# A second mixer whose values are the weights of its products, and ropes ahead of the weight halves, in a one-core encoder block

## The chip, the cores and the metric

One core of a Trainium2 chip runs the whole kernel in one launch. The metric is the device time of that launch in microseconds (us); lower is better.

## The reference, cut to what matters

One encoder block on 256 tokens of 1024 features. With n = RMSNorm(x), one wide projection gives queries, keys, values and gates of two attention mixers:

```python
[qA|kA|vA|qB|kB|vB|gA|gB] = n @ W_in
yA = DifferentialAttention(qA, kA, vA)      # 4 heads, rotary on 16 of 64 features, sub-norm
yB = softmax(SCALE * qB @ kB.T + bias) @ vB # 8 heads of 64 features, windowed by a bias
x = x + (sigmoid(gA) * (yA @ W_pA) + sigmoid(gB) * (yB @ W_pB)) @ W_out
x = x + PEER(RMSNorm(x))                    # 16384 experts, 16 of 256 candidates per head
out = RMSNorm(x)
```

The second mixer's softmax divides each row of exponentials by its sum before the product with the values; the kernel may divide before or after that product.

## The kernel before

**Work.** The weights come as a stream of 128-row tiles (128 partitions x 8 x 128 numbers, 512 KB each). Tile k is a slot: 0 to 3 are qA, 4 to 7 kA, 8 to 11 vA, 12 to 15 qB, 16 to 19 kB, 20 to 23 vB, 24 to 39 the gates (T_PROJ = 40), then 8 projections, 8 of W_out, 16 of the expert queries, 128 of expert inputs (U) and 128 of expert outputs (V). Every product is made of halves: ScalarE copies a raw tile to a rounded high half (`whi`, L475), VectorE subtracts it from the raw tile to get the low half (`wlo`, L699), and TensorE adds three products for each of 8 chunks, 24 matmuls of 256 columns a tile (L1156, one call of `tile`). The halves of tile t are made LEAD = 3 slots ahead, in slot t - 3, in a ring of 4. Tiles of values are taken in pairs (`token_pair`), 48 matmuls, and such a pair waits for the low halves of both of its tiles (L1330).

**Order.** Every engine's queue is an order written out by hand: a loop over the slots k, in which each engine's steps stand one behind another. An engine runs its queue strictly in that order, so a wait holds up all behind it.

- SyncE issues the loads (L377). Load t waits for the low half of tile t - 4 (L376).
- ScalarE, slot k: high half of tile k + 3 (L515), then for k < 8 the copy of the product of slot k out of PSUM (L519), which waits for that product. In slot 3 follow a square root (L521) and an exponential with a load of its table (L523). From slot 12 come the units' steps.
- VectorE, slot k < 12: low half of tile k + 3 (L818), then in slot 3 the norm (L716, L718), in slots 5, 6, 9 and 10 the four parts of the two ropes (L826; `ROPE_AT`, L79): part (0,0) makes two tables with cosine and sine times 1/rms (L806, L807), shuffles and multiplies (L809, L810), part (0,1) multiplies and adds (L812, L813), and (1,0) and (1,1) do the same for the keys. The queries' factor SCALE is in their tables.
- TensorE, slot k: the tile, then `scores`, `turn`, `times_v`. The first scores (slot 12) wait for both ropes (L1215).

**The opening.** `two_tiles` (L1276) runs tiles 0 and 1 in a mixed order as halves of x and weights arrive; tile 1's first product waits for the whole high half of tile 1 (L1307). In it, `rest(0, c)` are the products with the low half of x.

**Units.** Each mixer has 8 units (a head or pair of heads for 128 queries). Unit n starts in its slot: 12 to 19 for the first mixer, 25 to 32 for the second. In the second mixer, lag 0: scores on TensorE (L1221, two matmuls that use 64 rows of the array each), scale and bias and maximum on VectorE (L857, L860), exponentials with their sums on ScalarE (L550). Lag 1: 1/sum on VectorE (L846). Lag 2: four transposes of the probabilities (L1240) and their copy (L769). Lag 3: `times_v`, four matmuls with the turned probabilities as weights and 64 columns of values moving (L1258), result with queries on partitions, and VectorE multiplies it with 1/sum into `oB` (L774). In slots 37 and 38 (`Y_AT`, L88) `turn_y(2)` and `turn_y(3)` transpose `oB` (L1273, four transposes each), and `y_parts` makes halves `yhi`, `ylo` of it for the projections. The first mixer ends in `oA`, turned in slots 25 and 26.

An fp32 matmul shows as two records in the trace, a transpose as one.

## Time and profile before

| | |
|---|---|
| median of 3 runs | 1013.02 us (1012.43 to 1013.66) |
| the profiled execution | 1012.58 us |
| its span, first to last instruction | 1010.7 us |
| TensorE, matmuls | 1000.9 us busy, 99% |
| VectorE | 839.9 us, 83% |
| ScalarE | 604.9 us, 60% |
| mean granted TensorE clock | 0.998 of full speed |

The profiled execution's own time is 1.9 us above its span, which is what lies around the first and last instruction. Times in the rows below are us from the span's start. In a timeline, neighbouring instructions of one form are merged, and the bracket names the idle time of the engine ahead of them and what ended it. The chain is followed back from the last instruction through what released each step. Ends of matmuls are modelled, their starts are recorded.

### The profile page before, as it was taken

The numbers are of one execution on the slowest core, as the hardware profiler recorded it, in microseconds if no ns is written. First come the engines' busy times: TensorE is split into PE (matmuls) and PEld (weight loads), VectorE is DVE, ScalarE is ACT, GpSimd is POOL, SyncE is SP. The second block draws the span as 40 slices with busy tenths as digits, with TensorE's granted clock in tenths as the row PEclk, the third lists the DMA queues.
The fourth block names the chain that finished last, engine by engine and source line by source line (L and its number), as shares of the span: only waits on it lengthen the run. The fifth ranks groups of instructions, "written<-read, shape, count | busy, mean of one in ns | idle before, by whom it ended". The sixth has DMA issues, their size and how long they took to land.

```text
span 1010.7 us, 20524 instructions
## 1 busy us (share of the span) xinstructions
PE 1000.9 (99%) x6945; PEld 921.6 (91%) x6945; DVE 839.9 (83%) x1674; ACT 604.9 (60%) x1144; POOL 81.0 (8%) x38
## 2 busy tenths in 40 slices
PE   8999999999999999999999999999999999999997
PEld 8889999999999999999999999978888888888886
DVE  7888869769998989999999999777777777777776
ACT  6456544655545468888888888544444444444444
POOL 0000000277860000000000000000000000000000
PEclk9999999999999999999999999999999999999999
DMA  8744445645677766666666666887777777777772
GB/s 296 232 141 147 126 138 175 230 161 200 197 235 231 236 208 213 208 209 208 198 216 208 202 206 212 274 311 236 235 236 233 235 234 234 233 235 235 234 232 73
DMA packets 87749, 214.93 MB, mean 213 GB/s; under 512 B 9728, under 2 KB 43008, under 8 KB 87296
## 3 DMA queue, kind: packets, MB, share of 16 engines
q1 hardware_dynamic: 87104, 213.07, 65.3%
q8 instruction: 45, 0.74, 0.3%
q10 hardware_dynamic: 576, 0.93, 0.3%
q14 instruction: 24, 0.20, 0.1%
HBM read 195.08 MB, written 18.87 MB: 212 GB/s over the span
## 4 chain that ended last, share of the span: by engine, by line
PE 97%; DVE 1%; DMA 1%; issue 0%; ACT 0%; ACTq 0%
PE pO L1156 36%; PE pO L1441 18%; PE pTT L1473 17%; PE pM L1473 17%; PE pSS L1415 1%; PE pTT L1415 1%; DMA raw<-in_stream 1%; PE pSS L1221 1%; PE pSS L1379 1%; PE pM L1258 1%; PE pTT L1240 0%; PE pTT L1484 0%; PE pM L1252 0%; PE pTT L1233 0%; DVE wlos L699 0%
## 5 line engine op out<-in xcount | busy, mean ns | idle before, releaser
L475 ACT ACTIVATE whis<-raw 128x1024 fp32r<-128x1024 f32 x327 | 345.5, 1057 | 203.3 <-PE pM L1473 172.8
L1064 DVE TENSOR_TENSOR wlos<-raw,whis 128x1024 fp32r<-128x1024 f32 x125 | 153.3, 1226 | 87.5 <-ACT whis L475 87.4
L699 DVE TENSOR_TENSOR wlos<-raw,whis 128x1024 fp32r<-128x1024 f32 x169 | 205.1, 1219 | 14.7 <-ACT whis L475 14.2
L1156 PE MATMUL pO<-xhi,whis 128*128 128x256 f32 x752 | 212.2, 282 | 0.8 <-ACT qkT L519 0.8
L1156 PE MATMUL pO<-xlo,whis 128*128 128x256 f32 x752 | 210.0, 279 | 0.0
L1156 PE MATMUL pO<-xhi,wlos 128*128 128x256 f32 x752 | 209.8, 279 | 0.0
L1441 PE MATMUL pO<-xlo,whis 128*128 128x256 f32 x512 | 143.4, 280 | 0.0
L1156 PEld LDWEIGHTS pO<-xhi,whis 128*128 128x128 f32 x752 | 141.2, 188 | 2.2 <-issue 1.8
L1441 PE MATMUL pO<-xhi,wlos 128*128 128x256 f32 x512 | 143.0, 279 | 0.0
L1441 PE MATMUL pO<-xhi,whis 128*128 128x256 f32 x512 | 143.0, 279 | 0.0
L1156 PEld LDWEIGHTS pO<-xlo,whis 128*128 128x128 f32 x752 | 141.3, 188 | 0.0
L1156 PEld LDWEIGHTS pO<-xhi,wlos 128*128 128x128 f32 x752 | 140.9, 187 | 0.0
L602 ACT ACTIVATE ast<-pO 128x256 f32<-128x256 f32 x128 | 49.1, 384 | 100.5 <-PE pO L1156 69.6
L461 POOL TENSOR_TENSOR wlos<-raw,whis 128x1024 fp32r<-128x1024 f32 x33 | 80.6, 2447 | 216.2 <-ACT whis L475 216.1
L1441 PEld LDWEIGHTS pO<-xlo,whis 128*128 128x128 f32 x512 | 96.4, 188 | 0.0
L1441 PEld LDWEIGHTS pO<-xhi,wlos 128*128 128x128 f32 x512 | 96.1, 188 | 0.0
L1441 PEld LDWEIGHTS pO<-xhi,whis 128*128 128x128 f32 x512 | 95.9, 187 | 0.0
L610 ACT ACTIVATE ghot<-ghot,routeT 128x128 fp32r<-128x128 f32 x256 | 88.3, 397 | 5.4 <-DVE ghot L1043 5.4
L1055 DVE TENSOR_TENSOR wfull<-aring,G 128x256 f32<-128x256 f32 x128 | 78.9, 617 | 0.0
L1473 PE MATMUL pTT<-whis,ghi 128*128 128x512 f32 x250 | 78.7, 396 | 0.0
L1473 PE MATMUL pTT<-whis,glo 128*128 128x512 f32 x250 | 78.6, 396 | 0.0
L1473 PE MATMUL pM<-whis,glo 128*128 128x512 f32 x250 | 78.6, 395 | 0.0
(251 smaller groups left out, 1867.1 us busy)
## 6 DMA issues: line engine op xcount, KB each, us to landing
raw<-in_stream SPq DMA_DIRECT2D x199, 512.0 KB, 3.7
raw<-in_vrows SPq DMA_DIRECT2D x128, 512.0 KB, 3.5
a_scratch<-ast SPq DMA_DIRECT2D x128, 128.0 KB, 1.9
aring<-a_scratch SPq DMA_DIRECT2D x128, 128.0 KB, 3.3
biasm<-in_bias SPq DMA_DIRECT2D x8, 256.0 KB, 5.4
keysT<-in_keys SPq DMA_DIRECT2D x1, 1024.0 KB, 6.2
h_scratch<-h1tok SPq DMA_DIRECT2D x1, 1024.0 KB, 6.5
htok<-h_scratch SPq DMA_DIRECT2D x1, 1024.0 KB, 9.8
```

The source lines that it names most:

```text
L461: pool.tensor_tensor(wlo[s], raw[s][:], whi[s].bitcast(F32), ALU.subtract).then_inc(lo_ready, 1)
L475: act.activation(whi[s], raw[s][:], ACT.Copy).then_inc(hi_ready, 1)
L602: act.activation(ast[i % 2][:], pO[i % 2][:, 0:T], ACT.Gelu).then_inc(evac_act, 1)
L610: last = act.activation(ghot[:, u % HOTS, tok, 1, :], ghot[:, u % HOTS, tok, 0, :].bitcast(F32), ACT.Copy, scale=routeT[:, 2, at:at + 1])
L699: dve.tensor_tensor(wlo[t % RING], raw[t % RING][:], whi[t % RING].bitcast(F32), ALU.subtract).then_inc(lo_ready, 1)
L1055: dve.tensor_tensor(wfull[s % 2][:], aring[s][:], mine.rearrange("p t o -> p (t o)"), ALU.mult).then_inc(w_ready, 1)
L1064: dve.tensor_tensor(wlo[s], raw[s][:], whi[s].bitcast(F32), ALU.subtract).then_inc(lo_ready, 1)
L1156: last = pe.matmul(dst, st, mv, start=(c == 0 and q == 0), stop=(c == len(terms) - 1 and q == 2))
L1221: last = pe.matmul(pS[m][:, 0:T], qkT[rows, q0 + h, b * P:(b + 1) * P], qkT[rows, k0 + h, :], start=True, stop=True)
L1415: last = pe.matmul(pG[k % 2][:, p, tok * 2 * P:(tok + 1) * 2 * P], hot1[:, u % HOTS, tok, :], ghot[:, u % HOTS, tok].rearrange("p h i -> p ...
L1441: last = pe.matmul(pO[i % 2][:, 0:T], st[s][:, c, :], mv[:, c, :], start=c == 0 and q == 0, stop=c == C - 1 and q == 2)
L1473: last = pe.matmul(acc[b][q], st, mv[:, q * 512:(q + 1) * 512], start=first and n == 0, stop=n == 2 and (b, q) == closed)
```

## The change

It does seven things.

1. ScalarE makes the high half of tile 1 in two halves of four chunks, with a semaphore of its own for the first (`second_hi`), and TensorE starts tile 1 on the first. In `two_tiles` the `rest(0, c)` are spread otherwise (from chunk 5 on).
2. ScalarE's copy of product k goes ahead of the high half of tile k + 3, for product 0 ahead of the squares and of the high half of tile 3. It scales the queries of the first mixer by SCALE.
3. VectorE's rope parts go ahead of the low half of tile k + 3 in slots 5, 6, 9 and 10. The tables have no SCALE in them, and are made once, for the queries, and used again for the keys.
4. In the second mixer, ScalarE multiplies the probabilities with 1/sum in lag 1, two activations a unit, before they are turned. The transposes wait for them.
5. `times_v` of the second mixer has the values as weights (64 columns) and the turned probabilities moving (128 columns). The two heads of a pair write partitions 0 to 63 and 64 to 127, and alternate.
6. ScalarE copies that result from PSUM to `yhi` (in the slot after the product), and VectorE subtracts to `ylo` (`pair_low`), in place of the multiplication into `oB`.
7. `turn_y(2)`, `turn_y(3)` and their `y_parts` are gone.

```diff
@@ -85,7 +85,7 @@
 WHOLE_LAG = 2
 HALF = C // 2
 RCOL_AT = 6
-Y_AT = {T_GATE + 1: 0, T_GATE + 2: 1, T_PROJ - 3: 2, T_PROJ - 2: 3}
+Y_AT = {T_GATE + 1: 0, T_GATE + 2: 1}
 
 GTOK = 4
 GSUB = 2
@@ -506,17 +511,25 @@
             for c in range(C):
                 act.wait_ge(x_landed[c // 2], 16)
                 gained_hi(0, c)
-            hi_at(1)
+            def raw_copy(k):
+
+                act.wait_ge(tile_done, k + 1)
+                act.activation(qkT[:, k, :], pO[k % 2][:, 0:T], ACT.Copy, scale=SCALE if k < HA else 1.0).then_inc(evac_act, 1)
+
+            for half in range(2):
+                part = slice(half * HALF, (half + 1) * HALF)
+                act.wait_ge(raw_landed[1], 16)
+                act.activation(whi[1][:, part], raw[1][:, part], ACT.Copy).then_inc(hi_ready if half else second_hi, 1)
             hi_at(2)
+            raw_copy(0)
             act.activation(gates[:, 0:C // 2, :], xT[:, 0:C // 2, :], ACT.Square).then_inc(squares, 1)
             hi_at(3)
             for k in range(T_PROJ):
+                if 0 < k < T_VA:
+                    raw_copy(k)
                 if k:
                     hi_at(k + LEAD)
                 if k < T_VA:
-
-                    act.wait_ge(tile_done, k + 1)
-                    act.activation(qkT[:, k, :], pO[k % 2][:, 0:T], ACT.Copy).then_inc(evac_act, 1)
                     if k == 3:
                         rms_root(1)
                         act.wait_ge(lam_sums, 1)
@@ -537,6 +550,14 @@
                         act.wait_ge(pv_done, n + 1)
                         act.activation(gates[:, n // 2, n % 2 * P:(n % 2 + 1) * P], pM[n % 2][:, 0:P], ACT.Square, accum_out=ssA[:, 1, n:n + 1])
                         act.activation(oA[:, n // HA, n % HA, :], pM[n % 2][:, 0:P], ACT.Copy).then_inc(pv_taken, 1)
+                    else:
+                        act.wait_ge(pv_done, n + 1)
+                        act.activation(yhi[:, HA + (n - UNITS_A) % HA, (n - UNITS_A) // HA * P:((n - UNITS_A) // HA + 1) * P], pM[n % 2][:, 0:P], ACT.Copy).then_inc(yb_hi, 1)
+                for n in units_at(k, 1):
+                    if n >= UNITS_A:
+                        act.wait_ge(inverse_ready, n - UNITS_A + 1)
+                        for m in range(2):
+                            act.activation(prob[:, n % 2, m, :], prob[:, n % 2, m, :], ACT.Copy, scale=rz[:, n, m:m + 1]).then_inc(prob_normed, 1)
                 for n in units_at(k, 0):
                     act.wait_ge(max_ready, n + 1)
                     if n >= 2:
@@ -555,8 +576,7 @@
                 if k in Y_AT:
                     j = Y_AT[k]
                     act.wait_ge(y_full, j + 1)
-                    half, b = j // 2, j % 2
-                    act.activation(yhi[:, half * HA:(half + 1) * HA, b * P:(b + 1) * P], yf[:], ACT.Copy).then_inc(y_hi, 1)
+                    act.activation(yhi[:, 0:HA, j * P:(j + 1) * P], yf[:], ACT.Copy).then_inc(y_hi, 1)
             for k in range(T_PROJ, T_QUERY):
                 hi_at(k + LEAD)
                 if k == T_PROJ:
@@ -768,28 +788,23 @@
                 w = T if n < UNITS_A else 2 * T
                 dve.tensor_copy(probT[:, n % 2, 0:w], pT[n % 2][:, 0:w]).then_inc(turned_taken, 1)
 
-            def take_pv(n):
-                dve.wait_ge(pv_done, n + 1)
-                h, b = (n - UNITS_A) % HA, (n - UNITS_A) // HA
-                dve.tensor_tensor(oB[:, b, h, :].rearrange("p (m v) -> p m v", m=2),
-                                  pM[n % 2][:, 0:P].rearrange("p (m v) -> p m v", m=2),
-                                  rz[:, n, :].unsqueeze(2).to_broadcast([P, 2, DH]), ALU.mult).then_inc(pv_taken, 1)
+            def pair_low(n):
+
+                u = n - UNITS_A
+                dve.wait_ge(yb_hi, u + 1)
+                at = (slice(None), HA + u % HA, slice(u // HA * P, (u // HA + 1) * P))
+                dve.tensor_tensor(ylo[at], pM[n % 2][:, 0:P], yhi[at].bitcast(F32), ALU.subtract).then_inc(yb_lo, 1)
 
             def y_parts(j, t):
 
-                half, b = j // 2, j % 2
                 dve.wait_ge(y_turned, j + 1)
                 if j:
                     dve.wait_ge(y_lo, j)
-                src = pT[j % 2].rearrange("p (h t) -> p h t", h=HA)
-                if half == 0:
-                    dve.tensor_scalar(yf[:], src, lam[:, 6:7], None, ALU.mult).then_inc(y_full, 1)
-                else:
-                    dve.tensor_copy(yf[:], src).then_inc(y_full, 1)
+                dve.tensor_scalar(yf[:], pT[j % 2].rearrange("p (h t) -> p h t", h=HA), lam[:, 6:7], None, ALU.mult).then_inc(y_full, 1)
                 low_front(t)
                 dve.wait_ge(y_full, j + 1)
                 dve.wait_ge(y_hi, j + 1)
-                at = (slice(None), slice(half * HA, (half + 1) * HA), slice(b * P, (b + 1) * P))
+                at = (slice(None), slice(0, HA), slice(j * P, (j + 1) * P))
                 dve.tensor_tensor(ylo[at], yf[:], yhi[at].bitcast(F32), ALU.subtract).then_inc(y_lo, 1)
 
             bview = biasm[:].rearrange("p b h (r c) -> p b (h r) c", c=GRID_W)
@@ -802,9 +817,9 @@
                 turned = oB[:].rearrange("p b h v -> p (b h v)")
                 turned3 = turned.rearrange("p (h t) -> p h t", t=T)
                 if part == 0:
-                    scale = 1.0 if half else SCALE
-                    link(dve.scalar_tensor_tensor(tables[:, 0, :], K("cos"), scale, rstd[:], ALU.mult, ALU.mult))
-                    link(dve.scalar_tensor_tensor(tables[:, 1, :], K("sin"), scale, rstd[:], ALU.mult, ALU.mult))
+                    if half == 0:
+                        dve.tensor_tensor(tables[:, 0, :], K("cos"), rstd[:], ALU.mult)
+                        link(dve.tensor_tensor(tables[:, 1, :], K("sin"), rstd[:], ALU.mult))
                     dve.wait_ge(evac_act, (half + 1) * HA)
                     link(dve.stream_shuffle(turned, raws.rearrange("p h t -> p (h t)"), ROTATED))
                     link(dve.tensor_tensor(turned3, turned3, tables[:, 1, :].unsqueeze(1).to_broadcast([P, HA, T]), ALU.mult))
@@ -814,6 +829,8 @@
                     dve.wait_ge(roped, half + 1)
 
             for k in range(T_PROJ + 1):
+                if k in ROPE_AT:
+                    rope(*ROPE_AT[k])
                 if 0 < k < T_QB:
                     low_front(k + LEAD)
                 if k == 1:
@@ -822,8 +839,6 @@
                     rms(1)
                 if k == 5:
                     lambda_rest()
-                if k in ROPE_AT:
-                    rope(*ROPE_AT[k])
                 if k == RCOL_AT:
                     dve.wait_ge(rstd_turned, 1)
                     dve.tensor_copy(rcol[:], pTT[:, :, 0:1].rearrange("p b o -> p (b o)")).then_inc(rcol_ready, 1)
@@ -831,6 +846,9 @@
                     dve.wait_ge(tile_done, k + 1)
                     taken = qkT[:, k - T_QB + 8, :] if k < T_VB else gates[:, k - T_GATE, :]
                     dve.tensor_tensor(taken, pO[k % 2][:, 0:T], rstd[:], ALU.mult).then_inc(evac_dve, 1)
+                for n in units_at(k - 1, 3):
+                    if n >= UNITS_A:
+                        pair_low(n)
                 for n in units_at(k, 1):
                     dve.wait_ge(exp_done, 2 * (n + 1))
                     if n < UNITS_A:
@@ -843,7 +861,7 @@
                                                  ALU.mult, ALU.add).then_inc(dif_ready, 1)
                         dve.wait_ge(dif_ready, n + 1)
                     else:
-                        link(dve.reciprocal(rz[:, n, :], zs[:, n, :]))
+                        dve.reciprocal(rz[:, n, :], zs[:, n, :]).then_inc(inverse_ready, 1)
                 for n in units_at(k, 0):
                     dve.wait_ge(scores_done, n + 1)
                     if n < UNITS_A:
@@ -860,9 +878,6 @@
                         dve.tensor_reduce(nmx[:, n, :], prob[:, n % 2, :, :], AX_X, ALU.max, negate=True).then_inc(max_ready, 1)
                 for n in units_at(k, 2):
                     take_turned(n)
-                for n in units_at(k, 3):
-                    if n >= UNITS_A:
-                        take_pv(n)
                 if T_QB <= k < T_PROJ and k not in Y_AT:
                     low_front(k + LEAD)
                 if T_VB <= k < T_GATE:
@@ -1232,7 +1247,7 @@
                     for kb in range(TB):
                         last = pe.transpose(pT[n % 2][:, kb * P:(kb + 1) * P], dif[:, n % 2, kb * P:(kb + 1) * P], ident)
                 else:
-                    pe.wait_ge(exp_done, 2 * (n + 1))
+                    pe.wait_ge(prob_normed, 2 * (n - UNITS_A + 1))
                     if n < UNITS_A + 2:
                         pe.wait_ge(y_full, 2)
                     for m in range(2):
@@ -1242,8 +1257,10 @@
 
             def times_v(n):
                 pe.wait_ge(turned_taken, n + 1)
-                if n >= 2:
+                if 2 <= n < UNITS_A + 2:
                     pe.wait_ge(pv_taken, n - 1)
+                elif n >= 2:
+                    pe.wait_ge(yb_lo, n - 1 - UNITS_A)
                 last = None
                 if n == 0:
                     pe.wait_ge(evac_act, evac_engine(T_QB - 1)[1])
@@ -1253,24 +1270,19 @@
                                          start=kb == 0, stop=kb == TB - 1)
                 else:
                     pair = (n - UNITS_A) % HA
-                    for m in range(2):
-                        for kb in range(TB):
-                            last = pe.matmul(pM[n % 2][:, m * DH:(m + 1) * DH], probT[:, n % 2, m * T + kb * P:m * T + (kb + 1) * P],
-                                             vtok[:, kb, HA + pair, m * DH:(m + 1) * DH], start=kb == 0, stop=kb == TB - 1)
+                    for kb in range(TB):
+                        for m in range(2):
+                            last = pe.matmul(pM[n % 2][m * DH:(m + 1) * DH, 0:P], vtok[:, kb, HA + pair, m * DH:(m + 1) * DH],
+                                             probT[:, n % 2, m * T + kb * P:m * T + (kb + 1) * P], start=kb == 0, stop=kb == TB - 1)
                 last.then_inc(pv_done, 1)
 
             def turn_y(j):
-                half, b = j // 2, j % 2
-                if half == 0:
+                if j == 0:
                     pe.wait_ge(y_ready, 1)
                     pe.wait_ge(turned_taken, UNITS_A)
-                else:
-                    pe.wait_ge(pv_taken, UNITS_A + UNITS_B)
-                    pe.wait_ge(turned_taken, UNITS_A + UNITS_B)
-                src = oA if half == 0 else oB
                 last = None
                 for h in range(HA):
-                    last = pe.transpose(pT[j % 2][:, h * P:(h + 1) * P], src[:, b, h, :], ident)
+                    last = pe.transpose(pT[j][:, h * P:(h + 1) * P], oA[:, j, h, :], ident)
                 last.then_inc(y_turned, 1)
 
             def two_tiles():
@@ -1300,12 +1312,15 @@
                     pe.wait_ge(gain_hi, c + 1)
                     high(0, c)
                     low(0, c)
-                    if c >= C - 2:
-                        rest(0, c - (C - 2))
-                for c in range(2, C - 2):
+                    if c > HALF:
+                        rest(0, c - HALF - 1)
+                for c in range(C - HALF - 1, C - 2):
                     rest(0, c)
-                pe.wait_ge(hi_ready, 1)
                 for c in range(C):
+                    if c == 0:
+                        pe.wait_ge(second_hi, 1)
+                    elif c == HALF:
+                        pe.wait_ge(hi_ready, 1)
                     high(1, c)
                 for c in range(C - 2, C):
                     last = rest(0, c, c == C - 1)
@@ -1351,10 +1366,8 @@
                 if k == T_GATE + 1:
                     turn_y(0)
                     turn_y(1)
-                if k in (T_PROJ - 3, T_PROJ - 2):
-                    turn_y(k - T_PROJ + 5)
-            pe.wait_ge(y_lo, 4)
-            pe.wait_ge(y_hi, 4)
+            pe.wait_ge(y_lo, TB)
+            pe.wait_ge(yb_lo, UNITS_B)
             for k in range(T_PROJ, T_OUT):
                 tile_wait(k)
                 s = k % RING
```

The parts left out declare semaphores: `second_hi`, `inverse_ready`, `prob_normed`, `yb_hi` and `yb_lo`.

## Rows read from the trace of the kernel before

**Rows 1.** The page: span, and the chain that ended last, by engine.
```profile
span 1010.7 us, 20524 instructions
...
PE 97%; DVE 1%; DMA 1%; issue 0%; ACT 0%; ACTq 0%
```

**Rows 2.** Waits of TensorE: waiting line <- awaited line: us in total, times, longest.
```profile
PE pSS L1221 <- DVE qkT L813: 1.4, 1, 1.4
```

**Rows 3.** Timeline of TensorE, 0 to 50 us: start, duration, what, idle before.
```profile
13.69 0.36 PE L1156 MATMUL pO<-xhi,whis 128*128 128x256 f32 x1 [0.66 <-ACT qkT L519]
...
16.83 0.36 PE L1156 MATMUL pO<-xhi,whis 128*128 128x256 f32 x1 [0.18 <-ACT qkT L519]
...
47.52 0.70 PE L1221 MATMUL pSS<-qkT 64*128 64x256 f32 x4 [1.45 <-DVE qkT L813]
```

**Rows 4.** Timeline of ScalarE, 8 to 40 us, same columns.
```profile
17.84 1.06 ACT L475 ACTIVATE whis<-raw 128x1024 fp32r<-128x1024 f32 x1
19.84 0.38 ACT L519 ACTIVATE qkT<-pO 128x256 f32<-128x256 f32 x1 [0.93 <-PE pO L1156]
...
21.89 1.28 ACT L523 ACT_TABLE_LOAD   x1
...
23.30 1.04 ACT L475 ACTIVATE whis<-raw 128x1024 fp32r<-128x1024 f32 x1
```

**Rows 5.** Timeline of VectorE, 14 to 48 us, same columns.
```profile
14.69 1.22 DVE L699 TENSOR_TENSOR wlos<-raw,whis 128x1024 fp32r<-128x1024 f32 x1
...
18.73 2.35 DVE L699 TENSOR_TENSOR wlos<-raw,whis 128x1024 fp32r<-128x1024 f32 x2
...
24.44 2.38 DVE L699 TENSOR_TENSOR wlos<-raw,whis 128x1024 fp32r<-128x1024 f32 x2 [0.78 <-ACT whis L475]
...
30.84 1.22 DVE L699 TENSOR_TENSOR wlos<-raw,whis 128x1024 fp32r<-128x1024 f32 x1
31.98 1.22 DVE L812 TENSOR_TENSOR qkT<-qkT,mfull 128x1024 f32<-128x1024 f32 x1
33.23 1.23 DVE L813 TENSOR_TENSOR qkT<-qkT,oB 128x1024 f32<-128x1024 f32 x1
```

**Rows 6.** Chain that ended last, 20 to 50 us: start, duration, what.
```profile
32.21 5.72 PE pO L1156 x48
...
38.01 1.07 ACT whis L475
...
46.24 1.24 DVE qkT L813
```

**Rows 7.** Timeline of TensorE: the first matmuls and the last.
```profile
1.00 3.13 PE L1322 MATMUL pM<-ones 128*128 128x128 f32 x13 [1.00 <-POOL ones L456]
...
1005.08 0.28 PE L1484 MATMUL pO<-whis,glo 128*128 128x256 f32 x1
```

**Rows 8.** Window: PE, PEld, DVE, ACT, POOL busy, PEclk, DMA share, GB/s.
```profile
1007.00:1008.00 1.00, 0.00 (x0) 0.00 (x0) 0.54 (x1) 0.42 (x1) 0.00 (x0) 0.75 0.00 0
```

**Rows 9.** Chain that ended last, 94 to 152 us: tile, product, tile, turn.
```profile
100.26 2.92 PE pO L1156 x24
...
118.34 0.84 PE pM L1258 x8
119.18 2.88 PE pO L1156 x24
...
146.82 0.44 PE pTT L1273 x4
```

**Rows 10.** Chain that ended last, 52 to 66 us: scores, product, tile.
```profile
58.53 0.63 PE pSS L1221 x4
...
59.53 0.45 PE pM L1252 x4
59.98 2.73 PE pO L1156 x24
```

**Rows 11.** Timeline of ScalarE, 118 to 127 us: the wait ahead of the exponentials.
```profile
124.87 0.51 ACT L550 ACTIVATE prob<-prob,nmx 128x256 f32<-128x256 f32 x1 [2.59 <-DVE nmx L860]
```

More of the change, by code:

```diff
@@ L272, in build @@
         head_landed = sem("head_landed")
+        second_hi = sem("second_hi")
         head_hi = sem("head_hi")
@@ L320, in build @@
         y_lo = sem("y_lo")
+        inverse_ready = sem("inverse_ready")
+        prob_normed = sem("prob_normed")
+        yb_hi = sem("yb_hi")
+        yb_lo = sem("yb_lo")
         m_full = sem("m_full")
```

## The prediction

> **What bounds the kernel now.** I read the page first, for the span and the engines' shares of the chain that ended last; then the waits of TensorE, which show where that engine is not the bound; then the timelines of the first 50 us, where the change reorders queues; then the chain in the second mixer, where it changes matmuls. TensorE holds 97% of the chain [rows 1]. So whatever changes its own work or its waits passes to the end, one for one. Its longest wait is 1.4 us, at the first scores, for VectorE's ropes [rows 2]. The others are small and lie in the first 33 us [rows 3]. Less work on ScalarE or VectorE gains nothing by itself; a later half of a tile can cost.
>
> **Part 1, the opening.** Tile 2 starts at 13.69 after 0.66 of idle time, for ScalarE's copy of product 0, which stands behind the high half of tile 3 [rows 3]. With the copy ahead, and tile 1 started on its first four chunks, tile 2 could start at about 12.4. I take this as a gain of 1.3 us that doesn't last: tile 3 needs its low half, which VectorE begins at 14.69 for 1.22 us [rows 5], untouched by the edits. So tile 3 starts at about 15.95 and not 16.83 [rows 3], and 0.9 us is left. This is work ahead of the next wait, and is lost in it.
>
> **Part 2, copies ahead of high halves.** The high half of tile 6 starts at 17.84, the copy of product 3 at 19.84 [rows 4], 3.01 us after tile 3's start at 16.83 [rows 3]. In the new order the half stands behind that copy. Tile 3 starts at 15.95, so the copy runs at 18.96; 0.3 us on, the half runs from 19.25 to 20.3. VectorE makes two low halves (tiles 5 and 6) in 2.35 us from 18.73 [rows 5]; now the second waits, and ends at 21.5 in place of 21.0. Behind it come the norm, the root and the table load (before: 21.89 for 1.28 us), then the exponential and the copy of product 4 (0.3 us, now first), then the high half of tile 7, before at 23.30 [rows 4]. It moves by 0.5 + 0.3 = 0.8 us, to 24.1, and so does the low half of tile 7 behind it, from 24.44 [rows 5] to 25.24.
>
> **Part 3, ropes ahead of low halves.** From 24.44 to 34.5 VectorE has no idle time, so everything queued there adds up. The pair of tiles 8 and 9 needs the low half of tile 9, which runs from 30.84 to 32.06 [rows 5], and TensorE starts the pair at 32.21 [rows 6]. Now rope part (0,1) goes ahead of that half: two operations, 31.98 to 34.46, with the step between them 2.5 us [rows 5]. Rope (0,0) trades places with the low half of tile 8 and changes no sum. Low half of tile 9: 32.06 + 0.8 + 2.5 = 35.36; the pair starts at 35.5. TensorE is earlier until then: from 15.95 it has five tiles (3 to 7) of 2.73 to 2.92 us [rows 9, 10] and two small groups, so tile 7 ends at about 30.7. It would stand idle for 4.8 us, where its longest wait was 1.4 [rows 2]. Queued behind are all later tiles.
>
> The pair takes 5.72 us [rows 6], then come the second pair and tile 12. The first scores start at 47.52 after 1.45 us of idle time [rows 3], so from the pair's start to the end of tile 12 it is 47.52 - 1.45 - 32.21 = 13.86 us. New end of tile 12: 49.36. Are the ropes there by then? The high half of tile 12 follows the pair's end (before: 38.01, 5.80 after its start [rows 6]), so it runs at 41.3 to 42.35 and the low half to 43.6. Rope (1,0) has no tables now and is done before, since it stands ahead of that low half. Rope (1,1) takes 2.5 us like (0,1) (its last operation before: 46.24 [rows 6]), and ends at 46.1. So the scores don't wait: they start at 49.36 against 47.52 [rows 3], **+1.8 us**. The old wait of 1.45 us has gone, and a wait of 4.8 us stands in an earlier place.
>
> Loads: SyncE issues load t when low half t - 4 is done, so loads 13 to 15 go out about 3 us later. Their high halves, behind the pairs, move by as much. No DMA is added, and none is moved past another.
>
> **Part 4, the clock.** The last matmul starts at 1005.08 [rows 7], and in the window 1007 to 1008 the mean granted clock is 0.75 [rows 8]: it fell to the lower level (1.2 GHz) 2.1 us after TensorE stopped (half of that window at full speed, half at 0.5). At the start, the first 13 records of 128 columns took 3.13 us [rows 7], 0.21 each; four such records take 0.45 us later, 0.11 each [rows 10]. So after a cold start TensorE ran at half speed for 3 us. A stall of 1.45 us showed no such thing in its tiles. One of 4.8 us lies well above both, so I take it that the clock falls and that the pair begins with 3 us at 1.2 GHz: **+1.5 us** (bounds: 0, if it holds, and 2.9, half of the pair, if it stays low through it). With this, tile 12 ends at 50.9, the pair at 42.8, the ropes at 47.6: still ahead of the scores.
>
> **Part 5, the turns that go.** `turn_y(2)` and `turn_y(3)` are 4 transposes each, 0.44 us [rows 9], on the chain: **-0.9 us**. Their copies on VectorE and ScalarE were beside the tiles.
>
> **Part 6, values as weights.** Before: 8 records a unit, 0.84 us [rows 9]. After: 8 records of 128 columns. No row shows matmuls on two column halves. The nearest are the scores, on two row halves: 4 records of 256 columns in 0.63 us [rows 10]. By the 0.112 us of a 128-column record [rows 10], four in a row would be 0.90, two at a time 0.45; so they run two at a time, with 0.18 us for going in and out. For the new product: 4 x 0.112 + 0.18 = 0.63, and 0.04 more on the tile behind (2.92 behind scores, 2.88 behind the old product [rows 9]), 0.67. That saves 0.17 x 8 = **-1.4 us**. Lower bound, nothing for in and out: 0.45, -3.1 us. Upper bound, one column half after the other: 0.90 + 0.22 = 1.12, +2.2 us.
>
> **Part 7, the new steps beside TensorE.** ScalarE gets two 256-column activations a unit, 0.38 us each (the copy at 19.84 [rows 4]), and one of 128 columns, at most as much: 1.1 us. It waits 2.59 us in such a slot for VectorE's maximum [rows 11], and all three fit ahead of that. VectorE's `pair_low` replaces an operation of the same size. It waits for ScalarE's copy, and the scale and bias of the next unit are queued behind it; the copy has had a slot's time. The turn of a unit comes one slot after the scaling. I cost all of this at nothing. Were it all on the path, it would be 8 x 1.1 = 9 us, which the cover of 2.59 excludes.
>
> **Sum.** 1.8 + 1.5 - 0.9 - 1.4 = +1.0 us on the profiled execution's 1012.58: 1013.6. The median of the runs is 0.44 above that execution, so I say 1014.0 against 1013.02, which is +0.1%. A measurement of this kernel tells about 0.2% (2 us) from no change.
>
> **Rivals.**
>
> Slower: *the column halves take turns.* Place: the 8 products. Price: +2.2 in place of -1.4, total +4.6, 1017.6. It decides once a product costs 0.13 us more than I say, 0.80 against 0.67. For it: the scores' halves use different rows of the array, these share the rows. Against it: adjacent matmuls alternate between the halves, as in the scores. The Trainium skill bears on this in "TensorE: Matmul & The Clock Gate", Part 3: it says that a weight load overlaps with a running matmul only where the row group differs. By that rule each load of 64 columns stands open here, which by the page's P / 1.2 is 53 ns, 8 a unit, an estimate of 0.42 us a unit, and the total would be 8 x 0.42 above mine, +4.4. The same part reports gains from packing by columns, and no row of this trace can settle it.
>
> Faster: *the clock holds and tiles run short.* Some tiles of 24 matmuls last 2.73 us [rows 10] and others 2.83 to 2.9 [rows 9], 0.1 us apart, with no wait in either; every tile behind an old product was a long one. If those behind the new product were short, up to the end of the projections, that is 19 tiles, -1.9 us. Alone it gives -0.9, or 1012.1, no change. With a clock that holds (-1.5) it gives -2.4, 1010.6. Against the second part: the fall in rows 8 after 2.1 us.
>
> No change in another way: *the clock alone holds*, -0.5, 1012.5. That would follow if the stall were under 2 us, say if TensorE reached the pair later than I think.
>
> That the edits don't act as they say is a small risk: the opening's gain is real, and I hold that all of it is lost in the stall.
>
> **How the numbers follow.** Forecast and its neighbours within 2 us (clock falls or holds, columns in pairs): 0.51. Columns in turns or a longer spell of low clock: 0.32, slower. Short tiles with a clock that holds, or products near their lower bound: 0.17, faster. The range goes from the faster rival, 1010.6, to the slower one, 1017.6; the unchanged case alone is 1012.1 to 1015.
>
> **What would show it.** (a) An idle time of 4 to 5 us on TensorE ahead of the pair of tiles 8 and 9, ended by VectorE's low half at about 35.4; below 2 us would mean that I have VectorE's queue wrong. (b) Records twice as far apart for some 3 us behind it. (c) No wait at the first scores. (d) Tile 2 at about 12.4, tile 3 at about 16. (e) The new product in about 0.65 us, its records in pairs with nearly one start; single starts 0.11 apart would be the slower rival. (f) No turns at slots 37 and 38. (g) ScalarE's wait ahead of the exponentials shorter by about 1 us, and still there. I am wrong if the time is below 1011 or above 1017.6.

## The result, and the profile after

The changed kernel takes **1014.74 us** (median of 20, 1013.83 to 1015.32), the kernel before beside it 1013.0 (20 runs). The ratio is 1.0016, 95% interval 1.001 to 1.0023. The kernel became slower by 1.7 us, which is clear of the noise and within the 0.2% that the prediction called no change. The profiled execution took 1014.73 us, 2.15 more than the one of before.

The page: span, TensorE's busy time, engines of the chain.

```profile
span 1012.9 us, 20516 instructions
...
PE 1001.0 (99%) x6937; PEld 919.8 (91%) x6937; DVE 836.7 (83%) x1668; ACT 612.3 (60%) x1167; POOL 80.8 (8%) x38
...
PE 96%; DVE 2%; DMA 1%; ACT 1%; issue 0%; SPq 0%; DVEq 0%
```

Against [rows 1] the span is 2.2 us longer. TensorE's share of the chain fell from 97% to 96%.

The waits of TensorE (left out: 1.0 us ahead of its first matmul):

```profile
PE pO L1171 <- DVE wlos L719: 4.8, 2, 4.5
...
PE pO L1293 <- ACT xhi L492: 0.6, 1, 0.6
```

The wait of [rows 2], for the ropes at the first scores, is gone. In its place stand 4.8 us of waits for a low half of a tile, 4.5 of them at one place. The timelines show where. TensorE first: start, duration, what, and in brackets the idle time before it.

```profile
16.14 0.39 PE L1171 MATMUL pO<-xhi,whis 128*128 128x256 f32 x1 [0.36 <-DVE wlos L719]
...
35.68 0.55 PE L1171 MATMUL pO<-whis,xhi 128*128 128x256 f32 x1 [4.48 <-DVE wlos L719]
```

Tile 3 starts at 16.14 (before: 16.83 [rows 3]) and the pair of tiles 8 and 9 at 35.68 (32.21 [rows 6]). ScalarE in the same stretch:

```profile
19.27 0.38 ACT L517 ACTIVATE qkT<-pO 128x256 f32<-128x256 f32 x1 [2.10 <-PE pO L1171]
19.55 1.05 ACT L480 ACTIVATE whis<-raw 128x1024 fp32r<-128x1024 f32 x1
...
24.34 1.05 ACT L480 ACTIVATE whis<-raw 128x1024 fp32r<-128x1024 f32 x1
```

The copy of product 3 waits 2.10 us for its product, and the high half of tile 6 stands behind it: 19.55 where it was 17.84, and the half of tile 7 comes at 24.34, where it was 23.30 [rows 4]. VectorE:

```profile
20.64 1.23 DVE L719 TENSOR_TENSOR wlos<-raw,whis 128x1024 fp32r<-128x1024 f32 x1 [0.51 <-ACT whis L480]
...
25.49 1.23 DVE L719 TENSOR_TENSOR wlos<-raw,whis 128x1024 fp32r<-128x1024 f32 x1 [1.05 <-ACT whis L480]
...
31.79 1.23 DVE L827 TENSOR_TENSOR qkT<-qkT,mfull 128x1024 f32<-128x1024 f32 x1
33.05 1.23 DVE L828 TENSOR_TENSOR qkT<-qkT,oB 128x1024 f32<-128x1024 f32 x1
34.31 1.23 DVE L719 TENSOR_TENSOR wlos<-raw,whis 128x1024 fp32r<-128x1024 f32 x1
```

The low half of tile 7 starts at 25.49 (before 24.44 [rows 5]). The second rope part of the queries, 31.79 and 33.05, stands ahead of the low half of tile 9, which therefore runs from 34.31 and not from 30.84. That half is what the pair waits for.

Behind the stall comes the second cost. Windows of 1 us: the window, its length, then the busy time and count of TensorE, of its weight loads, of VectorE, ScalarE and GpSimd, then the mean granted clock, DMA share and GB/s.

```profile
35.00:36.00 1.00, 0.32 (x1) 0.35 (x2) 1.00 (x3) 0.00 (x0) 0.00 (x0) 0.80 0.02 8
36.00:37.00 1.00, 1.00 (x6) 1.00 (x6) 1.00 (x2) 0.00 (x0) 0.00 (x0) 0.50 0.56 82
...
38.00:39.00 1.00, 1.00 (x6) 1.00 (x6) 1.00 (x1) 0.00 (x0) 0.00 (x0) 0.50 1.08 334
39.00:40.00 1.00, 1.00 (x11) 1.00 (x10) 0.96 (x2) 0.00 (x0) 0.00 (x0) 1.00 1.01 191
```

The granted clock is 0.5 (1.2 GHz) when the pair starts, and until about 39.0. By their starts, the matmuls are 0.213 us apart until then and 0.118 us behind it. The chain through the rest of the opening:

```profile
35.68 15.87 PE pO L1171 x120
51.55 0.63 PE pSS L1236 x4
```

The first scores start at 51.48 by the timeline, 3.96 us later than the 47.52 of [rows 3]. Then the second mixer; the chain gives transposes, product, tile and scores of one unit, and the last run of tiles:

```profile
116.55 0.59 PE pTT L1255 x4
117.13 0.59 PE pM L1275 x8
117.72 3.02 PE pO L1171 x24
120.74 0.63 PE pSS L1236 x4
...
143.94 8.09 PE pO L1171 x67
```

The product takes 0.59 us and took 0.84 [rows 9], but the tile behind it takes 3.02 and took 2.88. The period of a slot is 4.83 against 4.94. After the last product there is no turn: `pO L1171` runs on without one.

A piece of the chain begins where the one before it ends, and these ends are modelled. The recorded starts of transposes, product and tile, before and after, divide the change otherwise:

```profile
117.68 0.66 PE L1240 MATMUL pTT<-cst,prob 128*128 128x128 f32 x4
118.17 1.00 PE L1258 MATMUL pM<-vtok,probT 128*128 128x64 f32 x8
118.99 0.37 PE L1156 MATMUL pO<-xhi,whis 128*128 128x256 f32 x1
```

```profile
111.65 0.66 PE L1255 MATMUL pTT<-cst,prob 128*128 128x128 f32 x4
...
112.82 0.39 PE L1171 MATMUL pO<-xhi,whis 128*128 128x256 f32 x1
```

From the product's start, 112.23 in the changed kernel, to the tile's it is 0.59 us and was 0.82, a gain of 0.23. From the first transpose's start to the product's it is 0.58 and was 0.49, a loss of 0.09 ahead of the product. Behind it the tile loses only about 0.02. The product's first records on TensorE, two that start together, and its weight loads with the next one behind them:

```profile
112.23 0.33 PE L1275 MATMUL pM<-probT,vtok 128*64 128x128 f32 x2
```

```profile
112.23 0.42 PEld L1275 LDWEIGHTS pM<-probT,vtok 128*64 128x64 f32 x8 [0.17 <-issue]
112.82 0.19 PEld L1171 LDWEIGHTS pO<-xhi,whis 128*128 128x128 f32 x1 [0.17 <-issue]
```

Eight loads of 64 columns lie in 0.42 us; each end of the group has 0.17 us in which no load runs, put down to issue. ScalarE's new steps in such a slot, and its wait ahead of the exponentials:

```profile
120.94 0.26 ACT L555 ACTIVATE yhi<-pM 128x128 fp32r<-128x128 f32 x1
121.62 0.91 ACT L560 ACTIVATE prob<-prob,rz 128x256 f32<-128x256 f32 x2 [0.43 <-DVE rz L864]
123.52 0.51 ACT L571 ACTIVATE prob<-prob,nmx 128x256 f32<-128x256 f32 x1 [0.98 <-DVE nmx L878]
```

The wait is 0.98 us, where it was 2.59 [rows 11]. The new steps take 0.26 and 0.91 us, and there is a new wait of 0.43 us for 1/sum. A wait is still left ahead of the exponentials, so these steps cost nothing at the end.

The balance of the profiled execution: +3.96 at the first scores, -0.11 in the first mixer's stage (second mixer's first scores: 98.92 us against 95.07), then about -0.9 for the products and -0.9 for the turns. The first product of the output stage starts at 177.81 against 175.73, 2.08 later, and the last matmul 2.14 later.

### The profile page after: what moved, and what is told of

The parts are those of the page before. It is cut to its first block, busy times and chain, and to the rows that moved or that the text cites. A ratio compares the mean times of both kernels' runs of the same rounds, so it can differ in the third digit from the quotient of the medians.

```text
span 1012.9 us, 20516 instructions
## 1 busy us (share of the span) xinstructions
PE 1001.0 (99%) x6937; PEld 919.8 (91%) x6937; DVE 836.7 (83%) x1668; ACT 612.3 (60%) x1167; POOL 80.8 (8%) x38
## 4 chain that ended last, share of the span: by engine, by line
PE 96%; DVE 2%; DMA 1%; ACT 1%; issue 0%; SPq 0%; DVEq 0%
PE pO L1171 36%; PE pO L1454 18%; PE pTT L1486 17%; PE pM L1486 17%; PE pSS L1428 1%; PE pTT L1428 1%; PE pSS L1236 1%; DVE wlos L719 1%; PE pSS L1392 1%; DMA raw<-in_stream 1%; PE pM L1275 0%; PE pTT L1255 0%; PE pTT L1497 0%; PE pM L1269 0%; PE pTT L1248 0%
## 5 line engine op out<-in xcount | busy, mean ns | idle before, releaser
L1171 PE MATMUL pO<-xhi,whis 128*128 128x256 f32 x752 | 212.2, 282 | 0.4 <-DVE wlos L719 0.4
L1171 PE MATMUL pO<-xlo,whis 128*128 128x256 f32 x752 | 210.0, 279 | 0.0
L1171 PE MATMUL pO<-xhi,wlos 128*128 128x256 f32 x752 | 209.8, 279 | 0.0
L1171 PEld LDWEIGHTS pO<-xhi,whis 128*128 128x128 f32 x752 | 141.1, 188 | 3.0 <-issue 2.0
L1171 PEld LDWEIGHTS pO<-xlo,whis 128*128 128x128 f32 x752 | 141.3, 188 | 0.0
L1171 PEld LDWEIGHTS pO<-xhi,wlos 128*128 128x128 f32 x752 | 140.9, 187 | 0.0
```

The costliest lines, as they stand in the source:

```text
L1171: last = pe.matmul(dst, st, mv, start=(c == 0 and q == 0), stop=(c == len(terms) - 1 and q == 2))
```

## The experiments

Each time stands beside the kernel before, run on the same chip: 1012.78 us for e1 to e4 and again for e7 to e9, 1012.85 for e5 and e6. The changed kernel's 1014.74 stands beside 1013.0, 0.2 us more, so a difference from it can be off by that much.

**e1: ropes back behind the low halves.**

```diff
-                if k in ROPE_AT:
-                    rope(*ROPE_AT[k])
                 if 0 < k < T_QB:
                     low_front(k + LEAD)
...
                 if k == 5:
                     lambda_rest()
+                if k in ROPE_AT:
+                    rope(*ROPE_AT[k])
```

> The changed kernel with the rope parts back behind the low halves; copies of the products stay ahead. Stall theory (VectorE's order makes the stall, and the stall makes the low clock): the pair of tiles 8 and 9 starts at about 33.4 us instead of 35.7, after some 2.4 us of idle time; the first scores come at about 47.8 instead of 51.5; time about 1011.5 if the clock holds, 1013 if it falls. Rival (the high halves that stand behind the copies are the cause): the pair stays at about 35.5 us and the time near 1014.7.

Measured: 1012.18 us, ratio 0.9988 (0.9978 to 0.9997). Two lines of TensorE's timeline, the pair and the first scores, then a window:

```profile
33.05 0.36 PE L1171 MATMUL pO<-whis,xhi 128*128 128x256 f32 x1 [2.06 <-DVE wlos L719]
```

```profile
47.37 0.70 PE L1236 MATMUL pSS<-qkT 64*128 64x256 f32 x4 [0.46 <-DVE qkT L828]
```

```profile
33.00:34.00 1.00, 0.95 (x8) 0.98 (x9) 1.00 (x1) 0.30 (x1) 0.00 (x0) 1.00 0.42 104
```

The idle time is 2.06 us, the pair starts at 33.05 and the first scores at 47.37. In the profiled execution the clock held; it took 1010.53 us. The ten executions lie in two groups, four from 1010.5 to 1011.0 and six from 1012.1 to 1012.6. The gap fits a clock that falls in some of them; their mean granted clocks point that way (0.998 to 1.0 in the four, 0.997 or 0.998 in the six) but overlap. So VectorE's order is the larger part of the stall, and the rival, the copies alone, is refuted.

**e2: the kernel before with ropes ahead, and nothing else.**

```diff
+                if k in ROPE_AT:
+                    rope(*ROPE_AT[k])
                 if 0 < k < T_QB:
                     low_front(k + LEAD)
...
-                if k in ROPE_AT:
-                    rope(*ROPE_AT[k])
```

> The kernel before with one edit, the rope parts ahead of the low halves. Stall theory: idle time of about 3 us ahead of the pair of tiles 8 and 9, which starts at about 34.7 us; 1.1 us later at the first scores if the clock holds, 3.2 us later if it falls to 1.2 GHz; time 1014.1 or 1016.2, I expect the latter. Rival (only ropes and copies together cost): no change, 1013.

Measured: 1015.17 us, ratio 1.0017 (1.0008 to 1.0027), 2.4 us more than the kernel before; ten executions, three from 1013.3 to 1013.6 and seven from 1015.0 to 1016.3. Timeline, then windows, of the profiled one (1015.05):

```profile
34.76 0.36 PE L1156 MATMUL pO<-whis,xhi 128*128 128x256 f32 x1 [3.26 <-DVE wlos L699]
```

```profile
35.00:36.00 1.00, 1.00 (x10) 1.00 (x10) 1.00 (x2) 0.00 (x0) 0.00 (x0) 0.86 0.37 53
36.00:37.00 1.00, 1.00 (x6) 1.00 (x6) 1.00 (x2) 0.00 (x0) 0.00 (x0) 0.50 0.89 295
```

Here the clock was still full when the pair started and fell 1 us later, at about 35.7, though TensorE was busy again. So one edit to one queue makes the stall and the low clock by itself. I had expected 1016.2; the median lies 1 us lower, and three executions, with a mean granted clock of 0.999, lie below the 1014.1 expected for a held clock. Behind the low clock come these starts, 95 steps apart:

```profile
39.17 0.28 PE L1156 MATMUL pO<-whis,xhi 128*128 128x256 f32 x1
...
49.95 0.28 PE L1156 MATMUL pO<-xhi,wlos 128*128 128x256 f32 x1
```

That is 0.1135 us a matmul, where the changed kernel had 0.118 behind its own low clock.

**e3: the stall filled.**

```diff
+                if k == T_VA - 1:
+                    for _ in range(18):
+                        pe.matmul(pM[1][:, 0:P], ones[:], ones[:], start=True, stop=True)
```

> The changed kernel with 18 matmuls on ones (128 columns, 4.0 us in all) in the stall behind tile 7; their result is used by nothing. The stall stays as long; only its emptiness goes. Clock theory: the granted clock stays at full speed and the pair's first 3.3 us aren't run at half speed: 1.7 us less, 1013.0 (1012.6 if the pair also runs at the shorter spacing). Rival (the time is lost to the wait alone and the low clock costs nothing at the end): 1014.7.

Measured: 1012.54 us, 2.2 less than the changed kernel's 1014.74; ratio 0.9997 (0.9988 to 1.0007), which makes it 1.9. Timeline and a window:

```profile
35.35 0.36 PE L1171 MATMUL pO<-whis,xhi 128*128 128x256 f32 x1 [0.46 <-DVE wlos L719]
```

```profile
36.00:37.00 1.00, 1.00 (x11) 1.00 (x10) 1.00 (x2) 0.00 (x0) 0.00 (x0) 1.00 0.57 111
```

The pair starts at 35.35, hardly earlier, the clock stays, and the first scores start at 49.13, 2.35 us ahead of the changed kernel. Of these, 0.33 are the earlier start of the pair. The low clock is 1.54: the changed kernel's first 15 matmuls of the pair took 3.33 us up to 39.01, and 15 at the full clock take 1.79 (here, from 35.35). The remaining 0.47 are the spacing of the 104 behind them, 0.118 us against 0.1135 here. That part isn't shown to come from the clock: in e2 the clock fell too, and the matmuls behind came at 0.1135. So matmuls that compute nothing, put into a wait, gave back more than half of what the front had lost, and the clock accounts for 1.54 of it.

**e9: the stall filled in part.** Against e3:

```diff
-                    for _ in range(18):
+                    for _ in range(6):
```

> As e3, but with 6 matmuls on ones (1.3 us), so that some 3.2 us of idle time are left ahead of the pair. If what counts is the idle time at a stretch, as in the kernel of e2 (3.26 us, the clock fell) and of e1 (2.06, it held), the clock falls in this one and the time stays near 1014.7. If any work in the stall keeps the clock, 1012.6.

```profile
35.31 0.55 PE L1171 MATMUL pO<-whis,xhi 128*128 128x256 f32 x1 [3.15 <-DVE wlos L719]
```

```profile
36.00:37.00 1.00, 1.00 (x7) 1.00 (x6) 1.00 (x2) 0.00 (x0) 0.00 (x0) 0.50 0.50 119
```

Measured: 1014.07 us (1012.48 to 1015.89), ratio 1.0012 (1.0003 to 1.0022). With 3.15 us idle the clock fell in the profiled execution, so that just any work in the stall doesn't keep it. The ten spread over 3.4 us: two have a mean granted clock of 0.999 or 1.0 and 1013.03 us or less, as if it held, and two 0.995 and 1015.24 or more. A stall left in part keeps the risk.

**e4: ropes and copies back**, so that the mixer's new form, the split opening and the shared tables are left. Beside e1's edit:

```diff
-                if 0 < k < T_VA:
-                    raw_copy(k)
                 if k:
                     hi_at(k + LEAD)
+                if 0 < k < T_VA:
+                    raw_copy(k)
```

> The changed kernel with ropes and, from slot 1 on, copies back in their old order: the second mixer's new form, the split opening and the key tables not made again are left. The mixer should give 0.9 us (turns) and 0.9 us (products), and the tables 0.9 us less of the wait at the first scores: 2.7 us less than before, 1010.3. Rival (the mixer's gain is lost elsewhere): 1012 to 1013.

Measured: 1010.0 us, ratio 0.9971 (0.9959 to 0.9982). TensorE's waits, without the first:

```profile
PE pO L1171 <- DVE wlos L719: 1.0, 1, 1.0
...
PE pO L1171 <- ACT qkT L517: 0.6, 1, 0.6
PE pSS L1236 <- DVE qkT L828: 0.5, 1, 0.5
```

The 1.45 us at the first scores became 0.5, by the 0.9 us of tables that aren't made twice. The copies ahead of the high halves are what e1 has beside this. With the clock held they cost 0.8 us: the first scores start at 46.52 against e1's 47.37, and e1's four fastest executions have a median of 1010.8. By the medians of all executions, 1010.0 against 1012.18, they cost 2.2. The changed parts that stand in the second mixer do give what they take out.

**e5: the two column halves one after another in the program.**

```diff
-                    for kb in range(TB):
-                        for m in range(2):
+                    for m in range(2):
+                        for kb in range(TB):
```

> The changed kernel with the second mixer's product in the other order of loops: both matmuls of the first column half, then both of the second, so that the halves no longer alternate. If the halves overlap only when neighbouring records use different halves: single starts 0.11 us apart, the product takes about 0.9 instead of 0.59 us, 8 times 0.3, 2.5 us more, 1017.2. If the hardware finds the pairs anyway: 1014.7.

Chain of one product and its tile, and the first records of a product:

```profile
117.82 0.59 PE pM L1275 x8
118.41 3.02 PE pO L1171 x24
```

```profile
117.75 0.34 PE L1275 MATMUL pM<-probT,vtok 128*64 128x128 f32 x2
```

Measured: 1015.27 us, ratio to the kernel before 1.0021 (1.0011 to 1.0031), against 1014.74 and 1.0016 for the changed kernel. The product takes 0.59 us and the tile 3.02, the same. Two records start together here too. The order in the program doesn't matter; my expectation of 0.9 us was wrong. The rest of the difference lies in the front, which the edit doesn't touch: the profiled execution stayed at the low clock until about 41.3, 5.5 us from the pair's start, not 3.3, and the first scores start at 52.16, 0.7 later. The times of both kernels overlap (1014.15 to 1015.69 here).

**e6 and e8: other places for ropes and copies.** To the changed kernel:

```diff
-ROPE_AT = {5: (0, 0), 6: (0, 1), 9: (1, 0), 10: (1, 1)}
+ROPE_AT = {6: (0, 0), 8: (0, 1), 9: (1, 0), 10: (1, 1)}
...
-                if 0 < k < T_VA:
+                if 0 < k < 3:
                     raw_copy(k)
                 if k:
                     hi_at(k + LEAD)
+                if 3 <= k < T_VA:
+                    raw_copy(k)
...
-                if k in ROPE_AT:
+                if k in (9, 10):
                     rope(*ROPE_AT[k])
                 if 0 < k < T_QB:
                     low_front(k + LEAD)
...
+                if k in (6, 8):
+                    rope(*ROPE_AT[k])
```

> The changed kernel with other places: the queries' rope parts in slots 6 and 8 behind the low half, the keys' in 9 and 10 ahead of it as changed, the copies ahead of the high half in slots 0 to 2 and behind it from slot 3. Stall theory: the low half of tile 9 is ready by about 29 us, no wait ahead of the pairs nor at the first scores, which come at about 44.8 us instead of 51.5; time about 1008.3, faster than both. Rival: VectorE's sum of work up to the ropes bounds the first scores wherever the parts stand, and they come at 47 us or later, 1010.5 or more.

> The same kernel as e6, for a firmer time beside the kernel before: 1007.8, ratio 0.995.

Measured: e6 1007.8 us (4 runs, 1007.61 to 1007.94), e8, the same kernel, 1007.81 (5 runs), ratio 0.9951 (0.9937 to 0.9964). Chain from tile 7 on, and TensorE's waits (but for the 1.0 us ahead of its first matmul, which all have):

```profile
28.10 16.45 PE pO L1175 x144
44.55 0.63 PE pSS L1240 x4
```

```profile
PE pO L1175 <- DVE wlos L721: 0.4, 1, 0.4
PE pO L1297 <- ACT xhi L492: 0.3, 1, 0.3
```

Six tiles, 144 matmuls, run in one piece, and the first scores start at 44.48 by the timeline, 7.0 us ahead of the changed kernel. The rival, that VectorE's work bounds them at 47 or later, is refuted. This version beats both, by 5.0 and 6.9 us.

**e7: the kernel before with e6's order alone.** The places of ropes and copies are e6's; the first copy, and nothing else of the changed kernel, moves ahead of the squares:

```diff
+            def raw_copy(k):
+                act.wait_ge(tile_done, k + 1)
+                act.activation(qkT[:, k, :], pO[k % 2][:, 0:T], ACT.Copy).then_inc(evac_act, 1)
...
             hi_at(2)
+            raw_copy(0)
             act.activation(gates[:, 0:C // 2, :], xT[:, 0:C // 2, :], ACT.Square).then_inc(squares, 1)
```

> The kernel before with only the order of e6: copies ahead of the high half in slots 0 to 2, the queries' rope parts in slots 6 and 8 behind the low half, the keys' in 9 and 10 ahead of it. Tile 1 isn't split, the mixer is as before, the tables are made twice. If the two parts add up, this is e6 plus the mixer's 1.8 us and some tenths for the tables: 1009.7, the first scores at about 44.8 us. Rival (the order only pays because the mixer's new form frees VectorE): 1011 or more.

Measured: 1010.19 us, ratio 0.9972 (0.9962 to 0.9983). The first scores start at 44.87. The order alone is worth 2.6 us, and e6 is 2.4 below e7: 1.8 from the second mixer's first scores on (91.93 against 92.62 there, 1000.25 against 1002.70 at the last matmul), and 0.7 ahead of it. So the two parts add up, and the rival is refuted. The tables made twice cost nothing here: TensorE doesn't wait for the ropes in e7 either. Of the 0.7, 0.2 stand at tile 3 (16.10 against 15.88), which the split opening can explain. The rest are matmuls at the wider spacing in e7, and a gap of 0.2 us ahead of its second scores whose cause the trace doesn't name. These also account for the 0.5 by which e7 lies above what I expected.

## Why the prediction was right, point by point

The sum was +1.0 us on the profiled execution, and it was +2.15; the median of 1014.0 came out as 1014.74, inside the range, slower as forecast. Two errors of one sign made the difference: the front cost 0.66 more and the products gave 0.5 less. The mechanism of each step was seen. Two things were luck. I had added 0.44 because the median of the kernel before lay that much above its profiled execution; in the changed kernel it lies 0.01 above, so the 0.44 covered a part of the 1.15 that the sum missed. And 0.47 of the front is a spacing of matmuls that no step of mine held. The range, 7 us wide, was no hard test; the signs (a) to (g) were.

- *Part 1, the opening.* Tile 2 started at 12.80, not 12.4, and tile 3 at 16.14, not 15.95, and the gain was lost in the stall. In e6, where no stall follows, tile 3 starts at 15.88 and the gain stays; e7, without the split, has it at 16.10, so most of it comes from the copies' order.
- *Part 2, copies ahead.* Predicted: the low half of tile 7 from 25.24; measured 25.49. e1 and e4 price the copies' place at 0.8 us with the clock held and at 2.2 by the medians.
- *Part 3, ropes ahead.* Predicted: idle time 4.8 us, the pair at 35.5. Measured: 4.48 and 35.68. e2 shows the ropes as a cause by themselves, e1 takes them away.
- *Part 4, the clock.* Predicted: 3 us at 1.2 GHz, 1.5 us. Measured: 3.3 us behind the pair's start, 1.54 us. e3 removes it without removing the stall. A part was missing: the matmuls behind came at 0.118 us and not at 0.1135, another 0.47 us up to the first scores. The clock isn't shown to be its cause. Together with part 3 the front was to cost 3.3 us and cost 3.96. Also missing: it isn't the same each time. Of the 20 executions 11 have a mean granted clock of 0.997 or 0.998 and a median of 1014.39, and 9 have 0.995 or 0.996 and 1015.13. The nine fit the longer low clock of e5's profile, whose mean is 0.995 too, but no trace of them was kept. They put the median 0.35 above that of the 11, about half of what it lies above my 1014.0.
- *Part 5, the turns.* -0.9, as said: no turn stands in the chain.
- *Part 6, the products.* The mis-sized term. I had -1.4; the period of a slot shrank by 0.11, 8 times, -0.9. The column halves do run two at a time, and the product itself takes 0.59 us, less than my 0.63. But I gave the tile behind 0.04 us more, from the tile behind the scores, and in the chain it takes 0.14 more. I had 0.18 us for going in and out, from the scores. By the recorded starts it is 0.24: 0.09 more between transposes and product, and 0.15 in the product's own 0.59, of which four turns of 0.11 are 0.44. The trace shows a gap of 0.17 us in the weight loads at each end of the group. The slower rival, halves in turn, is refuted, and e5 shows that not even the program's order brings it about. The Trainium skill's rule that a weight load overlaps with a running matmul only where the row group differs ("TensorE: Matmul & The Clock Gate", Part 3) isn't what this trace shows: the two halves share the row groups, and eight loads lie in 0.42 us beside the matmuls. I had written that no row could settle this, but plain tiles speak against it already. Each of their loads fills all 128 rows and takes 0.19 us, and yet the matmuls start 0.12 us apart; on the page TensorE is busy for 99% of the span and its weight loads for 91%.
- *Part 7, the new steps.* At no cost: ScalarE still waits 0.98 us in such a slot. That is 1.6 us less than before, not about 1, since it also waits 0.43 us for 1/sum.
- *The faster rival*, short tiles behind the new product, is refuted: the tiles behind the products got no shorter, and the projections take 22.53 us in both kernels (153.20 to 175.73 before, 155.28 to 177.81 now).

Why some tiles are 0.1 us longer than others, without a wait, stays open. What the timelines show is two spacings of the same matmuls, 0.1133 and 0.1177 us, both at the full clock and both in the kernel before (tile 3 has the one, tiles 4 to 6 the other); 24 times the difference is 0.1 us. The -0.11 of the first mixer's stage has that size: the tile behind the first scores came at 0.1177 before and at 0.1133 in the changed kernel. What chooses the spacing no run here was made for. The reason for the 0.17 us at the ends of the group stays open too.

## What to carry to other kernels

When a step is moved ahead in one queue, ask what becomes late behind it and which engine waits for that: here 2.5 us of ropes were put ahead of a half of a tile that TensorE needed, to remove a wait of 1.45 us that came later. A long stall of TensorE can cost more than its length: behind the 4.48 us here, matmuls ran at half the clock for 3.3 us, which cost 1.54. Then it pays to fill the stall or, better, to remove it. The mixer's rewriting was worth its 1.8 us, beside an order that cost 4.7 (1014.74 against e4's 1010.0); the same parts in other places made the kernel 5.0 us faster than before.

## What the runs showed of the hardware

- Idle times of TensorE and the clock in the profiled executions: 1.45 us (before) and 2.06 (e1), held; 3.15 (e9), 3.26 (e2) and 4.48 (the changed kernel), fell. In e2 it fell 1 us after the work had come back. The stay at 1.2 GHz was 3.4 us in three of these profiles, and 6.8 in e5's (idle for 4.48), 5.5 of them behind the pair's start. In e1, six of ten executions have times and mean clocks that fit a fall, though the profiled one held.
- Ten executions of e2 spread over 3.0 us, of e9 over 3.4. Without such a stall, eight of e7 spread over 0.4 and five of e8 over 0.6. But 28 of the kernel before, whose longest stall is 1.45 us, spread over 1.8 at mean clocks of 0.999 or 1.0, more than the changed kernel's 1.5 in 20, so the clock isn't the only source of scatter.
- Two fp32 matmuls with 64 weight columns each, on different halves of PSUM's partitions, run at the same time though they share the array's rows: eight of 128 moving columns take 0.59 us, in either order of issue, where eight in turn would take 0.90 by the 0.112 us of such a record.
